# The low part of one weight chunk in three made by ScalarE and an accumulating DMA, in the third FFN of a two-block model

## The reference

```python
def swiglu_ffn(x, w_gu, w_down):
    gate, up = jnp.split(x @ w_gu, 2, axis=-1)
    return (jax.nn.silu(gate) * up) @ w_down
...
x = layer_norm(DEEPNORM_ALPHA * x + swiglu_ffn(x, ffn_w_gu[i], ffn_w_down[i]), ln_g[i, 1], ln_b[i, 1])
```

## Time and profile before

| | |
|---|---|
| median of 3 runs | 1223.26 us (1222.88 to 1223.58) |
| the profiled execution, first to last instruction (its span) | 1221.8 us |
| its time outside the span | not recorded for itself; the median of the runs is 1.5 us above this span |
| TensorE busy | 1211.0 us, 99% |
| VectorE busy | 827.1 us, 68% |
| ScalarE busy | 647.3 us, 53% |
| POOL busy | 41.5 us, 3% |
| DMA traffic | 225.81 MB, mean 185 GB/s |

### The profile page before, as it was taken

How to read it: one execution, slowest core, us unless ns; L and a number is a source line. 1 busy time by engine, 2 the same in 40 slices (tenths; PEclk the granted TensorE clock), 3 DMA queues, 4 the chain that set the end, 5 groups by cost and what they waited for, 6 DMA issues and landing times.

```text
span 1221.8 us, 15988 instructions
## 1 busy us (share of the span) xinstructions
PE 1211.0 (99%) x6145; PEld 1019.5 (83%) x6145; DVE 827.1 (68%) x1190; ACT 647.3 (53%) x923; POOL 41.5 (3%) x85
## 2 busy tenths in 40 slices
PE   9999999999999999999999999999999999999997
PEld 7888888888787888888888888888888888888886
DVE  5987755756676666777547677667647777667753
ACT  7565644446666355556436554556534464556640
POOL 2000002100000000000010000000000000000000
PEclk9999999999999999999999999999999999999999
DMA  8676754754545556666647556566745444766551
GB/s 281 197 210 187 245 186 136 248 176 145 154 141 170 188 174 208 193 187 194 202 141 189 189 189 221 176 190 190 258 173 170 158 139 140 239 190 189 190 195 46
DMA packets 154747, 225.81 MB, mean 185 GB/s; under 512 B 8152, under 2 KB 85984, under 8 KB 154672
## 3 DMA queue, kind: packets, MB, share of 16 engines
q1 hardware_dynamic: 152144, 216.10, 55.7%
q0 software_dynamic: 2512, 8.69, 2.6%
q10 hardware_dynamic: 16, 0.00, 0.0%
HBM read 223.72 MB, written 1.05 MB: 184 GB/s over the span
## 4 chain that ended last, share of the span: by engine, by line
PE 96%; DMA 1%; DVE 1%; ACT 1%; issue 0%; SPq 0%; POOL 0%; DVEq 0%; ACTq 0%; POOLq 0%
PE ps L550 23%; PE ps L514 19%; PE ps L521 18%; PE ps L529 18%; PE ps L554 12%; PE ps L439 2%; DMA wgk<-in_gla_w_gk_dram 1%; PE ps L713 1%; PE ps L726 1%; DMA raw<-in_ff_w_gate_dram 0%; ACT wh L1000 0%; PE ps L929 0%; PE ps L696 0%; PE ps L899 0%; PE ps L655 0%
## 5 line engine op out<-in xcount | busy, mean ns | idle before, releaser
L1594 DVE TENSOR_TENSOR wl<-raw,wh 128x1024 fp32r<-128x1024 f32 x405 | 486.3, 1219 | 104.6 <-ACT wh L1000 101.8
L1000 ACT ACTIVATE wh<-raw 128x1024 fp32r<-128x1024 f32 x405 | 418.4, 1051 | 100.8 <-PE ps L529 42.1
L550 PE MATMUL ps<-XT,wh 128*128 128x512 f32 x1216 | 423.0, 392 | 0.0
L554 PE MATMUL ps<-XT,wl 128*128 128x256 f32 x1216 | 339.7, 279 | 0.0
L550 PEld LDWEIGHTS ps<-XT,wh 128*128 128x128 f32 x1216 | 227.6, 187 | 50.9
L554 PEld LDWEIGHTS ps<-XT,wl 128*128 128x128 f32 x1216 | 229.5, 189 | 0.2
L514 PE MATMUL ps<-wh,XT 128*128 128x512 f32 x510 | 203.3, 399 | 0.0
L521 PE MATMUL ps<-wl,XT 128*128 128x512 f32 x510 | 199.4, 391 | 0.2 <-DVE wl L2372 0.2
L529 PE MATMUL ps<-wh,XT 128*128 128x512 f32 x510 | 157.9, 391 | 0.0
L514 PE MATMUL ps<-wh,HHf 128*128 128x512 f32 x352 | 137.3, 390 | 0.0
L521 PE MATMUL ps<-wl,HHf 128*128 128x512 f32 x352 | 137.0, 389 | 0.0
(11 more groups left out here) (296 smaller groups left out, 1039.9 us busy)
## 6 DMA issues: line engine op xcount, KB each, us to landing
raw<-in_ffn_w_gu_dram SPq DMA_DIRECT2D x88, 512.0 KB, 4.3
raw<-in_w_in_dram SPq DMA_DIRECT2D x56, 512.0 KB, 4.1
raw<-in_ff_w_up_dram SPq DMA_DIRECT2D x44, 512.0 KB, 4.6
raw<-in_ff_w_down_dram SPq DMA_DIRECT2D x44, 512.0 KB, 4.6
raw<-in_ffn_w_down_dram SPq DMA_DIRECT2D x44, 512.0 KB, 4.6
raw<-in_ff_w_gate_dram SPq DMA_DIRECT2D x40, 512.0 KB, 4.1
raw<-in_gla_w_in_dram SPq DMA_DIRECT2D x24, 512.0 KB, 4.6
raw<-in_moba_w_in_dram SPq DMA_DIRECT2D x24, 512.0 KB, 4.8
```

The source lines that it names most:

```text
L550: e.matmul(o, wh_of(j)[:, w], XT[:, kt, :, :].rearrange("p a n -> p (a n)"), start=kt == 0, stop=False)
L554: ins = e.matmul(o[:, 0:256], wl_of(j)[:, w], XTH[:, kt, :], start=False, stop=kt == kts - 1)
L1000: e.activation(wh_of(j)[:, 0:m], raw[:, j % NR, 0:m], ACT.Copy).then_inc(S("wh"), 1)
L1594: e.tensor_tensor(wl_of(j)[:, 0:m], raw[:, j % NR, 0:m], wh_of(j)[:, 0:m].bitcast(F32), ALU.subtract).then_inc(S("wl"), 1)
```

## The change

In f3's narrow blocks, the chunks 1, 4, 7, ... 34 (12 of the 36) get their low part in another way. ScalarE, after the high part, writes the negative high part into the chunk's place in `wl` (a second activation with scale -1, semaphore wn). POOL then issues a DMA that adds the raw chunk to that place (`accum_op=ALU.add`), from SBUF to SBUF, and counts one of four semaphores wlo0 to wlo3. VectorE passes these chunks over. Everyone who waited for the low part of such a chunk waits for its DMA: TensorE before its first multiplication by it, and SP before it loads the chunk that takes the raw buffer over. POOL issues its 12 DMAs after it has issued the loads of gbc and bbc for f3's layer norm.

```diff
--- before.py
+++ after.py
@@ -231,6 +231,20 @@
             freed.append(last_use[i])
             last_use[i] = j
 
+        others = []
+        for c0, n in NARROW:
+            for part in "gu":
+                b, at, end, width, kts = blocks[f"f3{part}{c0}"]
+                others += range(at, end)
+        others = others[1::3]
+
+        def low_done(j):
+
+            if j in others:
+                i = others.index(j)
+                return S(f"wlo{i % 4}"), 16 * (i // 4 + 1)
+            return S("wl"), j + 1 - len([i for i in others if i < j])
+
         def wh_of(j):
             return wh[:, place[j], :] if place[j] < NS else wh2[:, place[j] - NS, :]
 
@@ -392,7 +406,7 @@
         def load_chunk(e, j):
             src, n, width, k0 = chunks[j]
             if j >= NR:
-                e.wait_ge(S("wl"), j - NR + 1)
+                e.wait_ge(*low_done(j - NR))
             e.dma_start(raw[:, j % NR, 0:n * width].rearrange("p (k n) -> p k n", k=n), src).then_inc(
                 S(f"raw{j % NR}"), 16)
 
@@ -517,7 +531,7 @@
                 if t == 0 and j < HALVES:
                     e.wait_ge(S("wl" if c else "wl_first"), j + 1)
                 elif t == 0 and c == 0:
-                    e.wait_ge(S("wl"), j + 1)
+                    e.wait_ge(*low_done(j))
                 e.matmul(o, lh[:, kt, rows(t)], low[:, w], start=False, stop=False)
                 if c + 1 == between[0]:
                     for stage, r, h in between[1]:
@@ -793,7 +807,7 @@
             b, at, end, width, kts = blocks["low"]
             o = ps[0:16, bank_of("low", 0), 0:256]
             e.wait_ge(S(f"ev{bank_of('low', 0)}"), ev_count["low", 0] - 1)
-            e.wait_ge(S("wl"), at + 1)
+            e.wait_ge(*low_done(at))
             for kt in range(8):
                 hw, lw = [w[:, kt * 16:kt * 16 + 16] for w in (wh_of(at), wl_of(at))]
                 e.matmul(o, hw, XTH[:, kt, :], start=kt == 0, stop=False)
@@ -998,6 +1012,8 @@
                         e.wait_ge(S("used"), freed[j] + 1)
                     e.wait_ge(S(f"raw{j % NR}"), 16 * (j // NR + 1))
                     e.activation(wh_of(j)[:, 0:m], raw[:, j % NR, 0:m], ACT.Copy).then_inc(S("wh"), 1)
+                    if j in others:
+                        e.activation(wl_of(j)[:, 0:m], raw[:, j % NR, 0:m], ACT.Copy, scale=-1.0).then_inc(S("wn"), 1)
                     at_chunk["next"] += 1
 
             def more():
@@ -1590,10 +1606,12 @@
                 while at_chunk["next"] <= min(last, len(chunks) - 1):
                     j = at_chunk["next"]
                     m = chunks[j][1] * chunks[j][2]
+                    at_chunk["next"] += 1
+                    if j in others:
+                        continue
                     e.wait_ge(S("wh"), j + 1)
                     e.tensor_tensor(wl_of(j)[:, 0:m], raw[:, j % NR, 0:m], wh_of(j)[:, 0:m].bitcast(F32),
                                     ALU.subtract).then_inc(S("wl"), 1)
-                    at_chunk["next"] += 1
 
             def more():
                 low_to(lead(at_chunk["step"] - 1))
@@ -2440,6 +2458,13 @@
                     e.tensor_tensor(rs[:, t:t + 1], rs[:, t:t + 1], mhalf[:, 0:1], ALU.pow).then_inc(S(f"rs{t}"), 1)
                     e.wait_ge(S(f"rs{t}"), stage)
 
+            def low_others():
+                for i, j in enumerate(others):
+                    e.wait_ge(S("wn"), i + 1)
+                    if i >= 4:
+                        e.wait_ge(*low_done(others[i - 4]))
+                    e.dma_start(wl_of(j), raw[:, j % NR, :], accum_op=ALU.add).then_inc(low_done(j)[0], 16)
+
             fill(ident[:, :], 0.0)
             keep(ident[:, :], ALU.not_equal, 0, 1, -1, P, 1.0)
             fill(mhalf[:, :], -0.5)
@@ -2518,6 +2543,8 @@
                 e.wait_ge(S("xg11"), stage - 2)
                 load_g(ln_g[i, k].partition_broadcast(P))
                 load_b(ln_b[i, k].partition_broadcast(P))
+                if stage == 6:
+                    low_others()
                 layer_norm(stage)
 
         blk = ctx.enter_context(nc.Block())
```

## The result

| | before | changed |
|---|---|---|
| median | 1223.12 us, 16 runs | 1226.35 us, 16 runs |
| lowest to highest | 1222.58 to 1225.12 | 1224.00 to 1228.96 |
| ratio | 1 | 1.0025, 95% interval 1.0018 to 1.0032 |
| span of the profiled execution | 1221.8 us | 1223.7 us |

The change makes the kernel 0.25% slower, some 3 us. The prediction had 1223.3 us; the time lies outside the 1221.9 to 1225.0 given for its likeliest case. It lies in the wide range of 1221.5 to 1243 only because that leaves room for two slow rivals, and what happened is neither of them, so that the range held by luck. Slower by more than 0.2% had a chance of 0.40.

What follows compares the result with a forecast made beforehand. TensorE was taken to bound the kernel, busy 99% of the span. 1221.8 us of span, 0 for VectorE, ScalarE, POOL, ring and the new wait, plus 1.5 us to the median, gave 1223.3 us, range 1221.5 to 1243.

Steps and rivals of the forecast that it cites:

- likeliest case: No change in the whole kernel's time within 0.2% (2.4 us), chance 0.56, own range 1221.9 to 1225.0 us.
- two slow rivals: Low parts landing too late for TensorE, chance 0.28, middle 1232 us; DMA engines filled by accumulations, chance 0.12, from 1240 up.
- What bounds the stage: In f3's narrow blocks TensorE alone sets the pace, 2.775 us a chunk, with 0.0 us idle before a matmul.
- VectorE's relief: VectorE loses 12 subtractions, 14.7 us, credited 0; rival that it counts: up to 14.7, likely 3 us faster, chance 0.04.
- ScalarE's and POOL's part: In the narrow blocks, 12 more activations (12.6 us) on ScalarE and 12 issues of 0.54 us on POOL: cost 0.
- L: Time from the accumulating DMA's issue to its landing, taken as 6.5 us; TensorE waits 0.
- The raw ring: SP's load of chunk c + 5 waits for the accumulation; ScalarE waits 0.2 to 1.2 us for chunk 15, absorbed: cost 0.
- it would limit from L = 10.3 on: A raw slot's path of load, two activations and accumulation takes 12.8 us against 16.65 us; it limits from 10.3 us landing.
- Late low parts: Rival: accumulations landing after 8.8 us stall TensorE; 1228.8 us at 9.9, 1239.3 at 12; chance 0.28, middle 1232.
- L - 8.8: TensorE's stall at each of chunks 10, 16, 22, 28 and 34 if the accumulation takes over 8.8 us.
- five stalls: Rival's sign: TensorE waits for the accumulation at chunks 10, 16, 22, 28 and 34; 5 x 1.1 = 5.5 us at 9.9.
- Full engines: Rival: an accumulation holds all 16 DMA engines beyond the free 3.2 us, so loads fall behind: 1257 us; chance 0.12.

Runs made afterwards that it cites:

- e1: The changed kernel with ScalarE's 12 negative high parts kept, but VectorE making these low parts from them, without DMA: 1223.18 us, ratio 1.0000.
- e3: The changed kernel with its 12 chunks loaded into three raw buffers of their own, so SP waits for an accumulation only nine chunks later: 1223.15 us, ratio 1.0002.
- e2: The kernel before, plus 12 accumulating DMAs by POOL into dead tiles that nobody reads or waits for: 1222.79 us, ratio 0.9997.
- e4: The changed kernel with the accumulation reading the raw chunk again from HBM, so SP waits only for ScalarE: 1226.08 us, ratio 1.0021.
- e7: The changed kernel with one chunk in two, 18 of 36 instead of 12: 1226.50 us, ratio 1.0029.
- e5: e2 with SP also waiting for the dead accumulation of chunk c before loading chunk c + 5; TensorE never waits for one: 1224.30 us, ratio 1.0013.
- e6: The changed kernel with ScalarE's two activations swapped, each accumulation issued 1 us earlier, and SP waiting for the high part too: 1224.18 us, ratio 1.0009.
- e10: The changed kernel with one chunk in six, 6 chunks instead of 12: 1222.79 us, ratio 0.9999.
- e9: The changed kernel measured once more, unaltered, side by side with e10: 1226.70 us, ratio 1.0034.
- e8: The changed kernel with one chunk in two (18) and three private raw buffers: 1224.71 us, ratio 1.0015.

## Why the prediction was right and wrong

*What bounds the stage: right.* TensorE's gapless steps, and VectorE's relief worth nothing. e1 and e3 leave the time alone while 12 subtractions are moved or dropped.

*ScalarE's and POOL's part: right at nothing* (e1, e2). An issue took 0.85 us on POOL instead of 0.54, and ScalarE's busy time grew by 10.4 us instead of 12.6; both hide all the same.

*L: right at the median,* 6.2 us against 6.5. The spread, 4.7 to 9.0, was not in the sum. The rows of before offered at most 5.9 us beside ordinary loads and 9.9 in a burst, and I took the burst to be somewhere else.

*The raw ring, "Cost: 0": this is the step that failed.* It followed one held load, chunk 15's, and let it land in 4.2 to 5.2 us. SP issues in order, so the loads of chunks 16 and 17 stood behind it, and all came out together when the accumulation landed. The next accumulation, one in every 8.3 us, then meets them. The landing times of 4.2 us had been measured with loads issued one at a time. The wait changed the very spacing on which they rested: 8.5 and 9.2 us for two of three loads, 9.0 for the accumulation. The bound "it would limit from L = 10.3 on" used 4.2 for the load. For chunk 19 the load took 8.5, and the path of load, two activations and accumulation ran from 798.8 to 817.3 us: 18.5 us, where the sum had 12.8 and the bound is 16.65.

*Late low parts, from L = 8.8: nearly right for one stall, the point wrong for the other.* An accumulation issued at 833.8 us took 8.9 us, and TensorE waited 0.3, where L - 8.8 gives 0.1. The larger stall had L = 7.6. Nor did five stalls recur at even distances. e4 shows what the pure case looks like.

*Full engines: the forecast's size right, the rival's wrong.* In 763 to 863 us POOL's queue holds ten accumulations:

```profile
q0 software_dynamic: 1498, 5.42, 28.7%
```

That is the 2.9 us of all engines for each that the prediction took, and the share of the stretch rose from 0.61 to 0.86 (about 0.95 forecast). e2 carries the change's traffic for nothing, and e7's share of 1.00 costs no more than the change.

What is shown: the loss is not ScalarE's work and not the traffic (e1, e2); SP's wait brings some of it with no other change (e5 against e2); taking that wait from recent accumulations, with three more buffers, removes it (e3); issuing 1 us earlier (e6) or half as often (e10) removes more than half or all. What stays open: e5 gave 0.13% of a loss of 0.25 to 0.34%, and I have not split the rest between TensorE's own wait on accumulations delayed by the ring and the differences between a dead and a real accumulation. Nor have I run the kernel with a deeper ring alone. That an accumulation issued close behind a load takes longer is read from the times of the transfers in the change and in e2; no experiment moves that distance alone.

No version beat the kernel before; e2's and e10's 1222.79 us are within their intervals of it. In a stage where VectorE isn't what TensorE waits for, there is nothing to win by relieving it.

## What to carry to other kernels

A wait for a slow transfer, placed on a queue that issues in order, holds everything behind it and lets it out as a burst; price it with the landing times of a burst that meets the next slow transfer, and not with those of evenly spaced transfers. Ask of every resource of the moved operation who gets it next: here the low part had 8.8 us and more at TensorE, but SP had been waiting for each source buffer before (39 waits in the stretch). When an operation moves to a slower path, give its source a buffer of its own, or space the transfers so that the queue drains between them.

## What the runs showed that I had not expected

A short stall of TensorE can cost twice. In e9's profile TensorE's weight loads waited 2.2 us for an accumulation at 834.6 us. Busy times in stretches of 2 us, the third number from the right being the granted clock:

```profile
833.00:835.00 2.00, 0.38 (x2) 0.38 (x3) 0.41 (x1) 0.33 (x1) 0.23 (x1) 1.00 0.76 155
835.00:837.00 2.00, 2.00 (x10) 1.72 (x9) 1.23 (x2) 1.12 (x2) 0.00 (x0) 0.65 1.00 177
837.00:839.00 2.00, 2.00 (x7) 1.71 (x7) 0.33 (x1) 0.07 (x1) 0.00 (x0) 0.50 0.96 303
839.00:841.00 2.00, 2.00 (x13) 1.71 (x13) 0.42 (x1) 1.07 (x2) 0.00 (x0) 0.99 0.89 242
```

After the stall the clock stood at the lower of its two levels, 1.2 GHz, until about 839 us, and a pair of matmuls took 0.64 us instead of 0.347. Six pairs, from 835.55 to 839.20 us, took 3.65 us instead of 2.08, so some 1.6 us came on top of the stall. The 1.6 us stall of the changed kernel's profile had no such sequel, nor had those of 1.5 and 1.6 us in e4, e7 and e8: their clock stayed at 1.00. In e9 the multiplications had stood 1.8 us. It may be part of the changed kernel's wide spread, 1224.0 to 1229.0 us over 16 runs. Two of these runs have a mean granted clock of 0.997, and they took 1227.3 and 1229.0 us; the eight with 0.999 have a median of 1225.9. Others with 0.999 took as much as 1227.6, so the clock is not the whole of it.
